# A mixture of experts whose token rows live in slots: one-hot gather of rows, sums and final norm by slot, indexed stores to the output

## What is computed

```
u2 = rmsnorm(h, norm_ffn)
p_group = softmax(t @ wg_r + bg_r)          # 4 groups, the best one is taken
top_v, top_i = top_k(expert logits in it, 2) # 2 of the group's 4 experts
for e in range(16):
    hid = silu(t @ w_gate[e]) * (t @ w_up[e])
    out = out + combine[:, e:e + 1] * (hid @ w_down[e])
h = h + out
return rmsnorm(h, norm_final)                # per token, over 1024 columns
```

## Time and profile before

| | us |
|---|---|
| timed runs | 1601.0, 1603.8, 1604.61 (median 1603.8) |
| the profiled execution's own time | 1600.88 |
| its span, first to last instruction | 1598.8 |
| PE busy | 1568.1 |
| DVE busy | 1136.1 |
| ACT busy | 856.6 |
| POOL (GpSimd) busy | 63.0 |
| four expert passes, from the first projection to the last matmul | 1294.9 to 1588.6 |

### The profile page before, as it was taken

One profiled execution on the slowest core, in us unless ns is written; L12 is line 12 of the kernel. 1 busy time (PEld: TensorE's weight loads), 2 busy tenths in 40 slices (PEclk: granted clock), 3 DMA queues, 4 the chain that ended last, 5 costly groups with the idle time before them and its releaser, 6 DMA issues.

```text
span 1598.8 us, 29124 instructions
## 1 busy us (share of the span) xinstructions
PE 1568.1 (98%) x11839; PEld 1470.1 (92%) x11839; DVE 1136.1 (71%) x1418; ACT 856.6 (54%) x1061; POOL 63.0 (4%) x53
## 2 busy tenths in 40 slices
PE   7999999999999999999999999999999999999998
PEld 7999998889999999998888999989999988888886
DVE  7655587776555765569777655578688688889887
ACT  5434455664344634345566444376544476767765
POOL 0000021000000000002100000020220000000000
PEclk9999999999999999999999999999999999999999
DMA  8666744146555576674315555646533669899992
GB/s 287 200 196 186 185 145 122 56 139 204 184 184 184 181 224 195 197 175 131 112 56 184 183 185 184 190 132 185 158 115 124 250 230 359 316 359 322 334 348 98
DMA packets 243781, 311.64 MB, mean 195 GB/s; under 512 B 51940, under 2 KB 183588, under 8 KB 243700
## 3 DMA queue, kind: packets, MB, share of 16 engines
q1 hardware_dynamic: 243088, 309.57, 60.3%
q10 hardware_dynamic: 612, 0.96, 0.2%
HBM read 306.97 MB, written 1.05 MB: 193 GB/s over the span
## 4 chain that ended last, share of the span: by engine, by line
PE 87%; DVE 6%; ACT 3%; DVEq 1%; issue 1%; DMA 1%; SPq 0%; ACTq 0%
PE psum L412 20%; PE psum L414 20%; PE psum L413 20%; PE psum L2763 4%; PE psum L2764 4%; PE psum L2765 4%; PE psum L2790 2%; PE psum L2789 2%; PE psum L2791 2%; DVE unit_low L404 2%; ACT unit_high L398 1%; PE psum L903 1%; PE psum L936 1%; PE psum L919 1%; PE psum L2703 1%; PE psum L1020 1%
## 5 line engine op out<-in xcount | busy, mean ns | idle before, releaser
L404 DVE TENSOR_TENSOR unit_low<-unit_raw,unit_high 128x2048 fp32r<-128x2048 f32 (+1 forms) x186 | 425.8, 2291 | 206.8 <-ACT unit_high L398 206.7
L398 ACT ACTIVATE unit_high<-unit_raw 128x2048 fp32r<-128x2048 f32 (+1 forms) x186 | 346.9, 1869 | 132.4 <-PE psum L414 127.6
L412 PE MATMUL psum<-UH,unit_high 128*128 128x256 f32 x1120 | 318.0, 284 | 2.9 <-DVE UL L458 1.1
L413 PE MATMUL psum<-UL,unit_high 128*128 128x256 f32 x1120 | 314.6, 281 | 0.0
L414 PE MATMUL psum<-UH,unit_low 128*128 128x256 f32 x1120 | 314.4, 281 | 0.0
L2485 DVE TENSOR_TENSOR unit_low<-unit_raw,unit_high 128x2048 fp32r<-128x2048 f32 x96 | 215.2, 2284 | 20.3 <-ACT unit_high L2481 20.3
L412 PEld LDWEIGHTS psum<-UH,unit_high 128*128 128x128 f32 x1120 | 211.5, 189 | 6.3 <-issue 3.9
L414 PEld LDWEIGHTS psum<-UH,unit_low 128*128 128x128 f32 x1120 | 211.6, 189 | 0.0
L413 PEld LDWEIGHTS psum<-UL,unit_high 128*128 128x128 f32 x1120 | 210.7, 188 | 0.1
L412 PE MATMUL psum<-U2H,unit_high 128*128 128x256 f32 x704 | 197.1, 280 | 1.4 <-DVE U2L L458 1.2
L414 PE MATMUL psum<-U2H,unit_low 128*128 128x256 f32 x704 | 196.3, 279 | 0.0
(11 more groups left out here) (512 smaller groups left out, 2918.9 us busy)
## 6 DMA issues: line engine op xcount, KB each, us to landing
unit_raw<-in_ffn_wg SPq DMA_DIRECT2D x44, 1024.0 KB
unit_raw<-in_ffn_wu SPq DMA_DIRECT2D x44, 1024.0 KB
unit_raw<-in_ffn_wd SPq DMA_DIRECT2D x44, 1024.0 KB
unit_raw<-in_w_in SPq DMA_DIRECT2D x32, 1024.0 KB
unit_raw<-in_expert_w_gate SPq DMA_DIRECT2D x32, 1024.0 KB, 6.9
unit_raw<-in_expert_w_up SPq DMA_DIRECT2D x32, 1024.0 KB, 8.0
unit_raw<-in_expert_w_down SPq DMA_DIRECT2D x32, 1024.0 KB, 6.2
unit_raw<-in_w_out SPq DMA_DIRECT2D x10, 1024.0 KB
```

The costliest lines, as they stand in the source:

```text
L398: act.activation(high[s][:, 0:w], raw[s][:, 0:w], ACT.Copy).then_inc(unit_high, 1)
L404: dve.tensor_tensor(low[s][:, 0:w], raw[s][:, 0:w], high[s][:, 0:w].bitcast(F32), ALU.subtract).then_inc(unit_low, 1)
L412: pe.matmul(dst, wh, xh, start=start, stop=False, skip_group_check=True)
L413: pe.matmul(dst, wh, xl, start=False, stop=False, skip_group_check=True)
```

## The change

The token rows are gathered once per pass as rows, with a plain one-hot, into `XSLOT` (the rows as they are) and, times the norm's factor, into `USLOT`, which PE transposes for the projections. The pass's result is added to XSLOT in slot form; squares, root and scaling by the final gain are done there in the next pass, and GpSimd (POOL) writes the 128 rows to their places in the output by an indexed store, with 4096 added to the index of a slot without a token, which the bounds check drops. The scatter, its split and the additions to tokens are gone. XTK is split once into XTH and XTL for the one-hot matmuls. The first pass still uses the old gather for its projections, and gathers its rows in step 2. The core of the diff:

```diff
...
-            for n in range(2):
-                mm = pe.matmul(psum[:, 3, n * P:n * P + P], POS0[:, n:n + 1].to_broadcast([P, P]), K[:, K_ID],
-                               start=(n == 0), stop=True, skip_group_check=True)
-            mm.then_inc(QM.sem, QM.inc("position_b"))
...
+        def one_hot_of(dve, positions):
+            for n in range(2):
+                ins = dve.tensor_scalar(ONE_HOT[:, n, :], K[:, K_IOTA], positions[:, n:n + 1], None, ALU.is_equal)
+            ins.then_inc(one_hot, 1)
+
+        def next_one_hot(dve, q):
+            dve.wait_ge(tok_gathered, 2 * q + 2)
+            dve.tensor_scalar(POSQ[:, :], POSQ[:, :], float(P), None, ALU.subtract)
+            dve.drain()
+            one_hot_of(dve, POSQ)
...
-        def scatter_pe(pe, q):
+        def rows_pe(pe, q, first=False):
+            pe.wait_ge(one_hot, q + 1)
+            if first:
+                pe.wait_ge(x_low, 2)
+            else:
+                pe.wait_ge(slot_copied, q)
             for half in range(2):
                 for n in range(2):
-                    for part, y in enumerate((YTH, YTL)):
-                        mm = pe.matmul(psum[:, SCATTER_B[n] + half, :], SELT[:, n * P:n * P + P], y[:, half * 512:half * 512 + 512],
...
+                    for part, x in enumerate((XTH, XTL)):
+                        mm = pe.matmul(psum[:, GATHER_B[half], :], ONE_HOT[:, n, :], x[:, n, half * 512:half * 512 + 512],
+                                       start=(n == 0 and part == 0), stop=(n == 1 and part == 1), skip_group_check=True)
+                mm.then_inc(tok_gathered, 1)
+
+        def turn_pe(pe, q):
+            for half in range(2):
+                pe.wait_ge(u_slot, 2 * q + (half - 1))
+                for kk in range(4):
+                    k = 4 * half + kk
+                    mm = pe.transpose(psum[:, TURN_B[half], kk * P:kk * P + P], USLOT[:, k * P:k * P + P], K[:, K_ID])
+                mm.then_inc(gathered, 1)
...
+                    if j == 3 and u == 0 and more:
+                        turn_pe(pe, q + 1)
...
-                if not first:
-                    slot_weights()
-                    scatter_pe(pe, q)
...
+                    if j == 2 and first:
+                        rows_pe(pe, 0, True)
                     down(g, j - 1, q, more)
                 if more:
                     transposes(3, q)
-                    gather_pe(pe, q + 1)
+                    slot_weights(q + 1)
+                    rows_pe(pe, q + 1)
                 down(g, 3, q, more)
...
-            scatter_pe(pe, last + 1)
...
+            def row_std_of(q):
+                for half in range(2):
+                    cols = slice(half * 512, half * 512 + 512)
+                    act.wait_ge(y_added, 2 * q + (half + 1))
+                    ins = act.activation(USLOT[:, cols], XSLOT[:, cols], ACT.Square, accum_out=SSQ[:, half:half + 1])
+                    if half == 0:
+                        ins.then_inc(row_sq, 1)
+                act.drain()
+                act.wait_ge(row_bias, q + 1)
+                act.activation(YSTD[:, 0:1], SSQ[:, 1:2], ACT.Sqrt, scale=1.0 / D, bias=YBIAS[:, :]).then_inc(row_std, 1)
...
                     high_step(j - 1, q, more)
                     silu_step(j, q, g)
+                    if j == 1 and not first:
+                        row_std_of(q - 1)
+                        act.activation(STD[:, 0:1], eps[:, :], ACT.Silu)
+                    if j == 3:
+                        if not first:
+                            act.wait_ge(rows_out, 16 * q if more else 64)
+                        act.wait_ge(tok_gathered, 2 * q + 2)
+                        act.activation(halves(XSLOT[:, :]), psum[:, GATHER_B[0]:GATHER_B[1] + 1, :], ACT.Copy).then_inc(slot_copied, 1)
                     for d in range(4, 6):
                         expert_high(act, q, g, base + d)
...
                 if more:
-                    evacuate_act(act, q + 1)
...
+                    act.wait_ge(slot_info, q + 2)
+                    for half in range(2):
...
+                        act.activation(USLOT[:, cols], psum[:, GATHER_B[half], :], ACT.Copy, scale=WSLOT[:, 0:1]).then_inc(u_slot, 1)
+                    expert_high(act, q, g, PASS_UNITS + 1)
+                    evacuate_act(act, q + 1, TURN_B)
...
-                act.activation(YTH[:, 0:512], psum[:, Y_B, :], ACT.Copy).then_inc(y_high, 1)
...
-                for n in range(0 if first else 2):
-                    add_dve(dve, q, n).then_inc(added, 1)
...
+                    for half in range(2):
+                        row_add(half)
...
-                    if j == 1 and more:
-                        select(dve)
-                    if j == 2:
-                        dve.tensor_scalar(SELT[:, :], POSB[:, :], K[:, K_IOTAC], None, ALU.is_equal)
...
+                    if j == 2 and not first:
+                        rows_of(q - 1, rows_ready)
...
+                    if j == 3:
+                        if not first:
+                            dve.wait_ge(rows_out, 16 * q if more else 64)
+                        ins = dve.tensor_scalar(ROWS[:, 0:1], WSLOT[:, 1:2], float(NOBODY), None, ALU.add)
...
+        def expert_pool(pool):
...
+                pool.tensor_tensor(XTL[:, n, :], XTK[:, n, :], XTH[:, n, :].bitcast(F32), ALU.subtract).then_inc(x_low, 1)
...
+                pool.indirect_dma_start(out[:, :], bass.IndirectOffsetOnAxis(ap=ROWS[:, column:column + 1], axis=0), XSLOT[:, :], None,
+                                        bounds_check=T - 1, oob_is_err=False).then_inc(rows_out, 16)
...
```

More of the change, by code:

```diff
@@ L311, in build @@
         POSQ = own("moe", "POSQ", [P, 2])
[L312 removed]
         SEL = own("moe", "SEL", [P, 2, P])
[L314 to L315 removed]
+        ONE_HOT = own("moe", "ONE_HOT", [P, 2, P], F32R)
+        WSLOT = own("moe", "WSLOT", [P, 6])
+        ROWS = own("moe", "ROWS", [P, 2], I32)
+        SSQ = own("moe", "SSQ", [P, 2])
+        YBIAS = own("moe", "YBIAS", [P, 1])
+        YSTD = own("moe", "YSTD", [P, 2])
         OH = own("moe", "OH", [P, 2, 4], BF16)
@@ L326, in build @@
         XTK = own("moe", "XTK", [P, 2, D])
-        YTH = own("moe", "YTH", [P, D], F32R)
-        YTL = own("moe", "YTL", [P, D], F32R)
+        XSLOT = own("moe", "XSLOT", [P, D])
+        USLOT = own("moe", "USLOT", [P, D])
         assert parts["moe"] <= YH_AT
@@ L2680, in router_dve @@
             dve.drain()
[L2681 to L2685, removed]
+            dve.tensor_copy(RT[:, :, 120], RS[:, 0:2])
+            for n in range(2):
+                dve.tensor_scalar(RT[:, n, 121:122], K[:, K_IOTAC], float(n * P - NOBODY), None, ALU.add)
+            dve.tensor_tensor(c(122, 126), c(112, 116), wide(118), ALU.mult).then_inc(EM.sem, EM.inc("comb"))
+            one_hot_of(dve, POS0)
         def select(dve):
@@ L2838, in one_pass @@
                 act.activation(STD[:, 0:1], eps[:, :], ACT.Silu)
+                if first:
+                    for n in range(2):
+                        act.activation(XTH[:, n, :], XTK[:, n, :], ACT.Copy).then_inc(x_high, 1)
                 silu_step(0, q, g)
@@ L2867, in expert_act @@
             act.activation(STD[:, 0:1], eps[:, :], ACT.Sqrt, bias=eps[:, :])
-            for n in range(2):
-                act.wait_ge(added, 2 * last + (n + 1))
-                act.activation(psum[:, 0:2, :], halves(XTK[:, n, :]), ACT.Square, accum_out=SS[:, n, 0:1])
-                act.drain()
-                act.activation(RS[:, 2 + n:3 + n], SS[:, n, 0:1], ACT.Sqrt, scale=1.0 / D, bias=eps[:, :]).then_inc(final_sq, 1)
+            row_std_of(last)
         def expert_dve(dve):
@@ L2891, in one_pass @@
                 expert_low(dve, g, 5)
-                dve.wait_ge(w_gathered, q + 1)
-                dve.tensor_copy(WSLOT[:, :], psum[:, W_B, 0:4])
-                dve.drain()
+                if first:
+                    dve.wait_ge(w_gathered, 1)
+                    dve.tensor_copy(WSLOT[:, :], psum[:, W_B, 0:6]).then_inc(slot_info, 1)
+                    dve.drain()
                 product(g, 0, q)
-                for n in range(0 if first else 2):
-                    add_dve(dve, q, n).then_inc(added, 1)
+                if not first:
+                    dve.wait_ge(unit_used, used(g, EU - 1))
+                    dve.wait_ge(slot_copied, q)
+                    for half in range(2):
+                        row_add(half)
                 for j in range(1, PER_GROUP):
@@ L3077, in _ @@
             expert_sp(sp)
-            for n in range(2):
-                for half in range(2):
-                    cols = slice(half * 512, half * 512 + 512)
-                    sp.wait_ge(out_ready, 2 * n + half + 1)
-                    sp.dma_start(out[n * P:n * P + P, cols], OTOK[:, n, cols]).then_inc(out_done, 16)
-            sp.wait_ge(out_done, 64)
         @block.tensor
```

150 lines of the change are left out of this document (96 added, 54 removed).

## The result

The changed kernel took 1623.6 us (median of 5 runs, 1621.87 to 1624.61) against 1603.96 (5 runs, 1601.0 to 1605.16) for the kernel before: recorded ratio 1.0131, interval 1.0118 to 1.0144 (the quotient of the two medians, 1.0122, lies in it). The forecast was 1614.3, its range ended at 1623. In the two traces the span grew by 22.4 us, where +10.55 was forecast.

What follows compares the result with a forecast made beforehand. It took PE, busy for 98% of the span, as the bound, with no slack in the expert step's loop through ACT's split and DVE's low part. Terms summed to +10.55 us; on the median 1603.8 that gave 1614.3, range 1608 to 1623.

Steps and rivals of the forecast that it cites:

- ACT's insertion, step 1: Passes 1 to 3: squares, root and two table loads between Silu and the next split delay PE, 3 x 4.3 = +12.9 us.
- XTL on POOL: Pass 0: two POOL operations of 2.4 us, wanted by PE only in step 2, so counted as free.
- XSLOT copy, step 3: All four passes: ACT's copy of 1024 columns from PSUM to XSLOT costs 4 x 0.9 = +3.6 us.
- scaling of rows, step 2: DVE's reciprocal and two row scalings delay the low part of unit 16, 3 x 0.4 = +1.2 us.
- work of PE: Pass boundaries: gathers become transposes, -8.07, and one more one-hot product, +1.97; sum -6.10 us.
- end of the passes: Passes 0, 1 and 2: one-hot work and the XSLOT copy make DVE's HL late for PE, 3 x 0.2 = +0.6 us.
- handover: Between passes: the longer chain through USLOT readies UL's first half about 0.15 us late for PE, 3 x 0.15 = +0.45.
- tail: After the last matmul: add, norm, scaling and indexed store (4.4) take 7.9 or 8.0 us against 10.2, so -2.2.
- Rival D: Each table switch on ACT also waits as long again as its load, 7.7 us more, 1622.0; chance 0.05.
- Rival A: The store lands late and ACT waits at the XSLOT copy in three passes, 1621 middling, 1641 worst; chance 0.14.
- Rival B: Faster: splits run ahead with over 4.35 us of slack behind Silu, hiding ACT's new work, 1597.8; chance 0.05.
- Rival C: No measurable change: step 1 stalls half as long and the tail at its best, +2.0 us; chance 0.04.

Runs made afterwards that it cites:

- experiment 2: Changed kernel with XTL made by DVE in step 2 of pass 0 instead of by POOL; 1617.8 us, ratio 1.0105.
- experiment 8: Changed kernel with squares, root and XSLOT copy ahead of ACT's copy of h, XTL on DVE, and rows scaled earlier; 1593.85 us, ratio 0.9955.
- Experiment 3: Changed kernel with 17 matmuls whose result nobody reads put into PE's step 1 gap in passes 1 to 3; 1617.76 us, ratio 1.0103.
- experiment 4: Changed kernel with a Square in place of the Sqrt in the passes, so no table loads there; 1610.51 us, ratio 1.0067.
- experiments 6: Changed kernel with the step 3 XSLOT copy and its wait for the store ahead of ACT's copy of h; 1623.07 us, ratio 1.013.
- experiment 7: Changed kernel with the XSLOT copy ahead of ACT's copy of h, and rows scaled before step 2's last two low parts; 1617.11 us, ratio 1.0093.
- experiment 5: Kernel before, with one-element Sqrt and Silu (two table loads) behind ACT's Silu in step 1 of passes 1 to 3; 1612.1 us, ratio 1.0059.
- experiment 1: Changed kernel with squares ahead of ACT's copy of h in step 1, root and table loads ahead of it in step 2; 1605.1 us, ratio 1.0026.

## Why the prediction was wrong in size

The direction, the main mechanism and its place were right: the step without slack, and ACT's new work in it. In the traces' 22.4 us the terms stand so:

| step | forecast | shown |
|---|---|---|
| ACT's insertion, step 1 | 4.35 each, +12.9 | 4.40 on ACT, 4.25 more on PE: +12.8 |
| half clock behind it | none | +6.8 |
| XTL on POOL | "Free" | +4.3 (pass 0, experiment 2) |
| XSLOT copy, step 3 | +3.6 | 0.9 + 3 x 0.8 = +3.3 |
| scaling of rows, step 2 | +1.2 | 0.27 + 0.28 + 0.66 = +1.2 |
| work of PE | -6.10 | -6.4 |
| end of the passes | +0.6 | +0.5 |
| handover | +0.45 | +0.7 |
| tail | -2.2 | -1.7 |

The last column was read from the starts of PE's matmuls in both traces. It adds up to 21.5 of the 22.4. The first pass starts 0.1 earlier, and the other 1.0 is made of delays of about 0.1 right behind the gaps and at the last transposes. In experiment 8 only small gaps remain, and its span is 6.7 under the kernel before, where -6.4, the tail's -1.7 and the +1.2 of pass end and handover make -6.9.

- **The first step that failed** is the "3 x 4.3 = +12.9". It priced the gap by its length alone. What PE paid is the gap and the matmuls behind it at 1.2 GHz, 19.6 us. The earlier trace rows show the clock at full only because that kernel never let PE wait here, so the trace of before could not give this price; it could have given the question. Experiment 3 shows that the two parts separate.
- **The second** is "Free: ... And XTL, two operations of 2.4 on POOL, wanted by PE in step 2". It asked only when PE wants the result, not what POOL's operation holds while it runs. Experiment 2 gives back the 4.3 us of pass 0.
- **The copies of XTH** on ACT, free in the forecast as well, are not what delayed DVE: in experiment 2 they are still there and the low part starts at 1305.38, against the forecast 1305.81.
- **The tail**: of the 4.4 for the store 4.9 are seen, from the scaling's end (1616.3) to 1621.2. The 3.2 that the Trainium skill, "DMA: Bandwidth & Descriptors", section "Anatomy of one DMA", gives is the landing of 3.2 that the last store has; the rest lies in POOL's start, 0.85 behind the scaling's end, and in 0.9 behind the landing. No row stood behind the 1.5 that the forecast put in for POOL; POOL's own row in the trace after, 0.97, lies within the landing.
- **Rival D** (each table switch waits as long again) would have given 1622.0, next to the measured time, and is refuted all the same: ACT's rows have 0.01 between a load and the next activation, and experiment 4 took back 2.69 for two loads, not the 5.1 of two loads at twice their length. The right time for the wrong reason.
- **Rival A** (the store is late) did not happen in the change, but the store landed up to 8.6 us after its start and not the 4.4 of the forecast, and of the room 0.35 and 0.1 us were left in passes 1 and 2; experiments 6 and 7 show what lay behind.
- **Rival B** (the splits are ahead) is refuted by experiment 5; its figure with every stall gone, 1595.5, is near what experiment 8 reached (1593.85), by moving the work to where ACT does have time. **Rival C** (half the stall) is refuted by the 4.25 that PE lost of the 4.35.

## What to carry to other kernels

An engine that is idle for 6 us of a step may still have no slack at one point in it: find for each inserted instruction the wait of the engine that it feeds, and place it ahead of the operand that the engine waits for anyway. A new stall of TensorE is priced with what runs behind it too: look in the windows for a fallen clock. Before calling work on GpSimd free, look at what VectorE does at that time, and before moving a consumer forward, look at what else it waits for.

## What the runs showed of the hardware

- Gaps that left PE idle for 2.83 and 4.09 us were followed by 3 to 6 us at 1.2 GHz, in all fifteen places of the five traces that have them, and cost 1.5 to 2.7 us more. The gap of 2.01 in pass 0, close behind one of 0.6 to 0.8, was followed by slow matmuls in five of six traces, and by none in experiment 4's; the three of 1.40 of that trace were followed by none. The fall doesn't come in the same amount each time: 13, 8 and 13 matmuls behind three equal gaps, and 4 runs of experiment 7's kernel had mean clocks of 0.990 to 0.995 and times of 1620.59 to 1614.14.
- The clock can fall at a place where nothing of the program differs. The windows view of experiment 1's kernel and of the kernel before, far ahead of the experts:

```profile
792.00:796.00 4.00, 3.60 (x17) 3.60 (x18) 2.53 (x12) 2.62 (x10) 0.00 (x0) 0.50 0.27 59
```

```profile
792.00:796.00 4.00, 3.85 (x33) 3.85 (x34) 2.75 (x13) 2.37 (x10) 0.00 (x0) 1.00 0.23 53
```

  In that execution the first projection of pass 0 came at 1297.38, in the kernel before's at 1294.89. An extra cost of 2 to 3 us fits the two levels of the kernel before and the spread of experiment 1, 1602.69 at 0.997 to 1608.74 at 0.994; that it is their cause is not shown, since of the kernel before only a run of the lower level has a trace.
- A GpSimd operation of 2.4 us on 1024 columns held up a VectorE operation of 0.19 until its own end, twice.
- An indexed store of 128 rows of 4 KB took POOL 0.97 to 2.58 us to issue and landed 3.2 us after its start in the tail, 4.8 to 8.6 beside the weight loads of the passes.
- A load of ACT's tables took 1.28 us and nothing around it, in each of the rows shown.
